# A cache page on 32 partitions, four neighbouring keys in each: three K and four V quads as buffers

## The reference

```
PAST_LEN, PAGE_SIZE, DEC_BATCH, DA_HEADS, DA_DK = 2048, 128, 8, 4, 64
...
k_past = cache_k[l][page_table].reshape(bd, past_len, DA_HEADS, 2, DA_DK)
v_past = cache_v[l][page_table].reshape(bd, past_len, DA_HEADS, DA_DV)
...
for k, v, kpos in segs:          # the past, then the new tokens
    s = jnp.einsum('bqhcd,bkhcd->bhcqk', q, k).astype(jnp.float32) * scale
    scores.append(jnp.where(kpos[None, :] <= qpos[:, None], s, NEG))
p = jax.nn.softmax(jnp.concatenate(scores, axis=-1), axis=-1)
a = p[:, :, 0] - lam * p[:, :, 1]
outs.append(jnp.einsum('bhqk,bkhd->bqhd', a[..., off:off + nk], v.astype(jnp.float32)))
```

## Time and profile before

| | |
|---|---|
| device time, median of 3 runs | 1909.88 us (1909.13 to 1913.38) |
| span of the profiled execution | 1912.5 us |
| PE busy | 1712.6 us, 90% |
| DVE, ACT, POOL busy | 573.6, 490.9, 170.8 us |
| DMA | 465.08 MB, mean 243 GB/s |
| K pages, V pages | 256 DMAs of 256 KB each, 4.6 us from issue to landing (median) |

### The profile page before, as it was taken

One profiled execution on the slowest core, in us unless ns is written; L12 is line 12 of the kernel. 1 busy time (PEld: TensorE's weight loads), 2 busy tenths in 40 slices (PEclk: granted clock), 3 DMA queues, 4 the chain that ended last, 5 costly groups with the idle time before them and its releaser, 6 DMA issues. The chain is left out here.

```text
span 1912.5 us, 34604 instructions
## 1 busy us (share of the span) xinstructions
PE 1712.6 (90%) x13666; PEld 938.0 (49%) x13666; DVE 573.6 (30%) x1596; ACT 490.9 (26%) x1046; POOL 170.8 (9%) x222
## 2 busy tenths in 40 slices
PE   6999998898896999999599999989888979999990
PEld 3457776674444333333244777666644543333330
DVE  2204635434225111110231154553331341111104
ACT  2012335654311000101111233555542100010012
POOL 1000002201000000000200000120020000000002
PEclk9999999998896999999799999999998969999995
DMA  8421039998734799999842200798897248999994
GB/s 276 161 76 53 15 102 306 307 333 284 272 136 168 256 368 388 400 394 388 295 155 84 95 1 23 236 317 297 285 308 275 103 159 317 386 386 397 399 365 162
DMA packets 215108, 465.08 MB, mean 243 GB/s; under 512 B 23137, under 2 KB 23138, under 8 KB 214946
## 3 DMA queue, kind: packets, MB, share of 16 engines
q1 hardware_dynamic: 197810, 402.40, 59.2%
q0 software_dynamic: 17136, 60.43, 8.3%
HBM read 429.10 MB, written 33.69 MB: 242 GB/s over the span
## 5 line engine op out<-in xcount | busy, mean ns | idle before, releaser
L960 PE MATMUL bank<-wslots,heads 128*32 128x512 f32 (+1 forms) x1568 | 314.6, 611 | 10.4 <-DVE heads L1677 5.5
L659 PE MATMUL bank<-xT,wslots 128*128 128x272 f32 x1024 | 241.8, 393 | 1.5 <-ACT heads L1220 0.8
L659 PEld LDWEIGHTS bank<-xT,wslots 128*128 128x128 f32 x1024 | 191.6, 190 | 40.7 <-issue 3.2
L960 PE MATMUL bank<-hgrn,heads 128*32 128x512 f32 (+1 forms) x736 | 197.2, 593 | 0.0
L613 PE MATMUL bank<-wslots,xT 128*128 128x512 f32 x384 | 174.1, 607 | 4.9 <-DMA wslots<-in_w_in 3.3
L710 PE MATMUL bank<-cst,wslots 128*128 128x128 f32 x1024 | 162.3, 287 | 14.5 <-ACT wslots L1270 6.4
L984 PE MATMUL bank<-wslots,temps 128*32 128x512 f32 (+1 forms) x768 | 169.7, 594 | 0.0
L960 PEld LDWEIGHTS bank<-wslots,heads 128*32 128x32 f32 (+1 forms) x1568 | 91.3, 119 | 159.9 <-issue 153.2
L710 PEld LDWEIGHTS bank<-cst,wslots 128*128 128x128 f32 x1024 | 115.1, 144 | 42.3 <-issue 35.7
L984 PE MATMUL bank<-hgrn,temps 128*64 128x512 f32 (+1 forms) x288 | 127.2, 595 | 1.8 <-DMA wslots<-in_w_down 1.1
L1830 DVE TENSOR_TENSOR temps<-temps,bank 128x512 f32<-128x512 f32 x26 | 17.9, 688 | 366.4 <-PE bank L960 366.4
(11 more groups left out here) (306 smaller groups left out, 2035.2 us busy)
## 6 DMA issues: line engine op xcount, KB each, us to landing
wslots<-in_cache_k SPq DMA_DIRECT2D x256, 256.0 KB, 4.6
wslots<-in_cache_v SPq DMA_DIRECT2D x256, 256.0 KB, 4.6
wslots<-in_w_gate SPq DMA_DIRECT2D x22, 2048.0 KB, 15.0
wslots<-in_w_up SPq DMA_DIRECT2D x20, 2048.0 KB, 16.4
wslots<-in_w_down SPq DMA_DIRECT2D x20, 2048.0 KB, 14.5
wslots<-in_w_in SPq DMA_DIRECT2D x14, 2048.0 KB, 9.8
hgrn<-in_w_up SPq DMA_DIRECT2D x12, 2048.0 KB, 15.6
hgrn<-in_w_down SPq DMA_DIRECT2D x10, 2048.0 KB, 13.3
```

What stands on the lines that cost most here:

```text
L659: x = mm(bank[6 + g % 2][:, 0:HALF], w[:, c, h * P:(h + 1) * P], xT[:, c, half * HALF:(half + 1) * HALF], start=(c == 0), stop=(c == DC - 1))
L960: x = mm(bank[2 + k][a:z, :], xeT[T_ % 2][:, c, a:z], weights((what, l, e), DC)[:, c, :], start=(c == 0), stop=(c == DC - 1))
```

## The change

A page's load now goes onto 32 partitions, each with four neighbouring keys, 8 KB in a row of main memory; the four pages of a quad lie on partitions 0-31, 32-63, 64-95 and 96-127. A "page" that PE turns is then every fourth key of all four pages of the quad: index `s % 4` of the quad's tile, so PE waits for the whole quad (64 counts of one semaphore) before the first of its four turns and for nothing before the other three. K has three buffers of a quad in place of eight of a page, and K quad g waits until all of quad g - 3 has been turned. V has four buffers of a quad in place of five. The third K buffer lies where the first V buffer was. The tiles of x have semaphores of their own.

```
-        kpage = [w_a[:, 4096 + 512 * s:4096 + 512 * (s + 1)].rearrange("p (h n) -> p h n", h=H) for s in range(8)]
-        vquad = [w_a[:, o:o + 2048].rearrange("p (j h n) -> p j h n", j=4, h=H) for o in (8192, 10240, 12288, 0, 2048)]
-        NK, NV = len(kpage), len(vquad)
+        kquad, vquad = ([w_a[:, o:o + 2048].rearrange("p (j h n) -> p j h n", j=4, h=H) for o in at_]
+                        for at_ in ((4096, 6144, 8192), (10240, 12288, 0, 2048)))
+        NK, NV = len(kquad), len(vquad)
...
-        kl = [sem(f"x_tile_then_k_page_loaded{i}") for i in range(NK)]
+        xl = [sem(f"x_tile_loaded{i}") for i in range(NT)]
+        kl = [sem(f"k_quad_loaded{i}") for i in range(NK)]
...
-                    def load_page(page, dst, cache, done):
-                        sp.dma_start(dst.rearrange("p h n -> p (h n)"),
-                                     cache[l, bass.ds(page, 1)].rearrange("o p h n -> (o p) (h n)")).then_inc(done, 16)
-
-                    sp.wait_ge(*last_use(("in", l, 3)))
+                    def load_pages(pages, dst, cache, done):
+                        for j in range(4):
+                            sp.dma_start(dst[32 * j:32 * j + 32].rearrange("p k h n -> p (k h n)"),
+                                         cache[l, bass.ds(pages[j], 1)].rearrange("o (r k) h n -> (o r) (k h n)", k=4)).then_inc(done, 16)
+
                     ids = None
                     for g in range(NQ + 1):
                         previous, ids = ids, four_pages(g) if g < NQ else None
-                        for p in range(4 * g, min(4 * g + 4, DB * NPG)):
-                            if p >= NK:
-                                sp.wait_ge(kt_ps, l * DB * NPG + p - NK + 1)
-                            load_page(ids[p % 4], kpage[p % NK], t_in["cache_k"], kl[p % NK])
+                        if g < NQ:
+                            if g < NK:
+                                sp.wait_ge(*last_use(("in", l, (3, 3, 4)[(l * NQ + g) % NK])))
+                            G_ = l * NQ + g
+                            if G_ >= NK:
+                                sp.wait_ge(kt_ps, 4 * (G_ - NK) + 4)
+                            load_pages(ids, kquad[G_ % NK], t_in["cache_k"], kl[G_ % NK])
                         if g:
                             v = l * NQ + g - 1
                             if g <= NV:
 
-                                sp.wait_ge(*last_use(("in", l, (4, 4, 5, 6, 6)[v % NV])))
+                                sp.wait_ge(*last_use(("in", l, (4, 5, 6, 6)[v % NV])))
                             else:
                                 sp.wait_ge(pv_ps, vn(v - NV) + 1)
-                            for j in range(4):
-                                load_page(previous[j], vquad[v % NV][:, j], t_in["cache_v"], vl[v % NV])
+                            load_pages(previous, vquad[v % NV], t_in["cache_v"], vl[v % NV])
...
-                pe.wait_ge(kl[s % NK], 16 * (int(s % NK < NT) + l * (DB * NPG // NK) + s // NK + 1))
+                q = g // 4
+                if s % 4 == 0:
+                    pe.wait_ge(kl[q % NK], 64 * (q // NK + 1))
...
-                    x = tr(bank[s % 2][:, h * P:(h + 1) * P], kpage[s % NK][:, h, :], ident)
+                    x = tr(bank[s % 2][:, h * P:(h + 1) * P], kquad[q % NK][:, s % 4, h, :], ident)
```

## The result

The changed kernel takes 2146.36 us (median of four runs, 2143.06 to 2149.41), against 1911.63 us of the kernel before beside it: a ratio of 1.1226, 95% interval 1.1203 to 1.1248, so 235 us slower. The forecast was slower by 174 us, 2084 us with a range up to 2140; the sign and most of the mechanism came out, the size lies just outside the range.

The account below looks back on a forecast made before the run. PE and DMA were taken as almost balanced in the page stages. Slower page loads and an empty queue once a batch gave +83 us, GpSimd's transfers +4, a layer: 1909.9 + 174 = 2084 us, range 1950 to 2140.

Parts of the forecast that it names:

- The pace of pages on 32 partitions: Page stages: page loads run at 225 GB/s, between bounds of 219 and 386, so a quad takes 4.66 us.
- The sum: Layer 0's page stage: batches of 41.9 us for 29.9, +87 us a layer, +174 for two, 2084 us.
- the price of the V wait: Once a batch the DMA queue runs empty until slot 20 is through: 2.5 plus 2.1, together 4.6 us.
- the slow clock: Rival: PE idles in the page stage, its clock falls; 25 us a layer, 2134 us; chance 0.2 for over 2120.
- the likeliest case: Page stages: loads at 205 to 250 GB/s, 2040 to 2120 us in all; chance 0.5.
- GpSimd's state transfers: Page stage: 7.7 us of all DMA engines, some in the empty time, so 4 us a layer added.
- the 593.2 worked out: End of layer 0's page stage, in us, for 510.2 before: +83.
- The rival of full overlap: Page stages: a quad's pages overlap at 386 GB/s, PE sets 28.7 us a batch, 1896 us; chance 0.1.
- Later quads of the batch wait for values already past: Page stages: only a batch's first V load waits for values; later ones do not hold up SP.
- Half overlap: Rival, page stages: engines share their way half the time, 280 GB/s, 1984 us; chance 0.2 for 1925 to 2040.
- K's waits and buffers: Page stages: fewer semaphore waits of PE cost nothing; 12 K pages for 8 do not help the V wait.
- PE busy about 0.6: Sign in the page stage: PE busy about 0.6 of it, waiting at every fourth page turn for K.

Follow-up runs that it names:

- the first experiment: The changed kernel with each page back on 128 partitions, its buffers, waits and SP's order kept: 2011.81 us, ratio 1.051.
- V later: The changed kernel, pages on 32 partitions, but SP issues V one quad later (K quad g, then V quad g - 2): 2040.23 us, ratio 1.0689.

## Why the prediction was right or wrong

**The pace of pages on 32 partitions** was right in mechanism and nearly in size: 225 GB/s taken, 222 in a full stretch. That it is the neighbouring partitions is shown by four runs that keep everything else: 2 KB packets there are as slow as 8 KB, 64 neighbours have 240 GB/s (and 32 with halves in turn 237), 32 spread ones run near full pace, 128 restore it. With V later and only the layout different, the layout costs 2040.23 - 1915.97 = 124 us. The sum had 119 for it (174 less 2 x 6 x 4.6 for the turnarounds).

**The step that failed is the price of the V wait**, "Together 4.6" for a batch, 55 us in the sum. The V order alone costs 2146.36 - 2040.23 = 106 us on 32 partitions, and 2011.81 - 1915.97 = 96 on 128. The mechanism was named rightly (K behind the waiting V load, the queue empty until slot 20 is through). What was mis-sized is seen in the profile of layer 0, the stage by busy time and the DMA queues of 302.7 to 585.1 us:

```profile
300.00:640.00 340.00, 227.32 (x2782) 146.56 (x2781) 90.91 (x275) 118.54 (x250) 34.61 (x44) 0.79 0.84 196
```

```profile
q1 hardware_dynamic: 9216, 50.34, 80.8%
q0 software_dynamic: 1040, 3.41, 4.1%
```

The empty stretch is 7.0 us in the batch shown, with PE's three steps at a granted clock of 0.59, 4.7 us for 2.5. Where the clock was 0.98, in the second gap, 4.7 us were empty, as in the sum; where it was lower, 5.0 to 8.6 (the longest follows a wait of PE for a state of HGRN). I had the slow clock as a rival of its own (2134 us); it was a part of the likeliest case, because PE idled a third of this stage and was granted 0.79, for 0.96 before. Its terms on top of the sum at 219 GB/s (2098) would have given 2148; that this is so near 2146 is luck in part, since it has 14 us for a tail that came 5.5 later. Over six batches, 302.71 to 585.08, a batch took 47.1 us for 41.9: the empty engines 6.5 for 4.6, the pages 0.808 x 282.4 / 6 = 38.0 for 37.3, GpSimd's state transfers on the same engines 0.041 x 282.4 / 6 = 1.9, for which the sum had 4 a layer or 0.7 a batch, and 0.7 for the rest. For those states PE waited 7.1 us in three places. That is 6 x 5.2 = 31 us a layer; the tail (45.8 us from 585.08 to 630.9, for 40.3) adds 5.5 and the start 1.2: together the 37.7 by which the stage ended later than the 593.2 worked out. The 106 us that the order costs are 8.8 a batch; what it costs beyond the empty engines of the gaps is not taken apart by any run.

**The rival of full overlap** (1896 us, the V wait costing 2.6 us of PE a batch) is refuted twice. Pages hardly overlap, and at full pace (the first experiment) the V wait still costs 96 us. "Later quads of the batch wait for values already past" did not hold either: SP had issued its K quad by 314.35 and its next V load only at 320.01, two such waits a batch; the second cost no empty engines here (share 0.96). The rival's sum had taken the K quad to land 7.5 us after the values; in the first experiment it came after 10.7, because SP issues the four V loads, the page numbers and the four K loads one after the other, 6.4 us that the sum priced at nothing. **Half overlap** did not come: the order of the change gains 1 to 2% over 219 GB/s.

**K's waits and buffers** at nothing: nearly right for three K quads (1916 for 1910 with everything else undone). **PE busy about 0.6**: 26.24 of 40, and 227.32 of 340 us in the stage, so 0.66. What stays open is how much of the turnaround the clock alone costs; the trace shows the longer instructions, but no run held the clock up.

## What to carry to other kernels

Before laying a load on fewer partitions to get longer packets, look for any transfer in the trace that already has that shape and compare its time per packet with its neighbour's: a 32-row output of 0.7 us told the pace of 67 MB a layer. Buffers are not lookahead by themselves: in one issue order, what counts is what stands behind the load that waits, and a change of a few lines in that order was worth 106 us, nearly the 124 of the pages' pace. When a stage starts to wait for loads, price the compute in its turnarounds at the slow clock too: here the granted clock was under 0.8 in four gaps of six.

## What the runs showed of the hardware

32 partitions four apart take 8 KB packets at 393 ns on average where 32 neighbours take 600, so a small number of partitions is no limit by itself. Loads to alternating halves gain 7% (237 for 222 GB/s), not two times. With addresses from registers SP needs 1.8 to 2.9 us for four page loads on 128 partitions, and from a V quad to the next K quad 1.6 us more, in which it loads page numbers (334.36 + 2.86 to 338.77). Both together are 4.4 us there, where the kernel before took 29.9 / 16 = 1.9 us for a page slot.
